# Column sums, head transposes and a part copy put in another order in a hand-scheduled fp32 two-block network

## What is computed

```python
# first block, first mixer
p = (h @ w_in)                    # 256 x 5120, in 10 blocks of 512 columns
f = lb + (1 - lb) * sigmoid(hf)
o_hg = hgrn2_scan(silu(hq), 1 - f, log(f), hi)   # decay exp(bcum_t - bcum_s) for every pair of rows
o_ret = retention_scan(rope(rq), rope(rk) * 128 ** -0.5, rv)
...
# second block
z = h @ w_in                      # 256 x 5120, again 10 blocks of 512 columns
q, k, v, xb, bg, cg, gates = split(z)
q = partial_rope(rms_norm(to_heads(q), g_q), cos, sin)   # 8 heads of 64
k = partial_rope(rms_norm(to_heads(k), g_k), cos, sin)
y_a = moba_attention(q, k, v)
...
x = x + ga2 * hierarchical_moe(h2, ...)   # 32 experts, 6 MB of fp32 weights each
```

## Time and profile before

| | us |
|---|---|
| median of three executions | 1425.47 |
| lowest and highest | 1422.99, 1425.79 |
| the profiled execution, own time | 1423.28 |
| its span, first to last instruction | 1421.5 |
| PE busy (share of the span) | 1229.7 (87%) |
| DVE busy | 651.7 (46%) |
| ACT busy | 245.9 (17%) |
| POOL busy | 59.9 (4%) |
| mean granted clock of TensorE | 0.94 |

### The profile page before, as it was taken

How to read it: one execution, slowest core, us unless ns; L and a number is a source line. 1 busy time by engine, 2 the same in 40 slices (tenths; PEclk the granted TensorE clock), 3 DMA queues, 4 the chain that set the end, 5 groups by cost and what they waited for, 6 DMA issues and landing times.

```text
span 1421.5 us, 15723 instructions
## 1 busy us (share of the span) xinstructions
PE 1229.7 (87%) x6651; PEld 807.0 (57%) x6651; DVE 651.7 (46%) x874; ACT 245.9 (17%) x501; POOL 59.9 (4%) x74
## 2 busy tenths in 40 slices
PE   8999999999999999999999999999674564645647
PEld 5889749994457676997445888655231221312212
DVE  7598326667865754567876764314110100101001
ACT  2331312220012321331002242013000000000000
POOL 1005100000010001000001200000000000000000
PEclk9999999999999999999999999999986887878888
DMA  9533335449953334556993443397999999999997
GB/s 359 179 129 118 119 133 192 158 170 346 350 190 119 118 119 149 178 179 232 348 350 112 167 148 123 130 430 299 424 428 428 428 429 427 428 427 428 428 425 264
DMA packets 94392, 376.98 MB, mean 265 GB/s; under 512 B 7248, under 2 KB 7920, under 8 KB 82416
## 3 DMA queue, kind: packets, MB, share of 16 engines
q1 hardware_dynamic: 93728, 373.84, 67.8%
q0 software_dynamic: 576, 2.10, 0.4%
q10 hardware_dynamic: 16, 0.00, 0.0%
HBM read 374.88 MB, written 1.05 MB: 264 GB/s over the span
## 4 chain that ended last, share of the span: by engine, by line
PE 74%; DMA 21%; DVE 2%; ACT 2%; issue 1%; POOL 0%; DVEq 0%; SPq 0%; ACTq 0%; POOLq 0%
PE PS L740 17%; PE PS L1004 14%; PE PS L957 12%; PE PS L783 9%; DMA weights<-in_w 8%; DMA arena<-in_w 6%; PE PS L1220 6%; DMA proj_rows<-in_w 4%; PE PS L723 4%; PE PS L1258 3%; DMA normalised<-in_w 2%; PE PS L992 2%; PE PS L679 2%; PE PS L865 1%; PE PS L925 1%
## 5 line engine op out<-in xcount | busy, mean ns | idle before, releaser
L740 PE MATMUL PS<-weights,normalised 128*128 128x256 f32 x816 | 182.6, 380 | 2.0 <-DVE weights L1820 1.3
L1220 PE MATMUL PS<-weights,x_rows 128*32 128x512 f32 x368 | 132.4, 726 | 47.1 <-DMA proj_rows<-in_w 25.1
L740 PEld LDWEIGHTS PS<-weights,normalised 128*128 128x128 f32 x816 | 153.8, 190 | 26.3 <-issue 5.1
L1004 PE MATMUL PS<-weights,arena 128*128 128x512 f32 x384 | 167.4, 592 | 0.0
L2420 DVE TENSOR_TENSOR x_rows<-x_rows,PS 128x512 f32<-128x512 f32 x8 | 8.4, 1046 | 289.2 <-PE PS L1220 289.2
L1220 PE MATMUL PS<-arena,x_rows 128*32 128x512 f32 x256 | 95.2, 707 | 39.3 <-DMA weights<-in_w 28.5
L783 PE MATMUL PS<-weights,arena 128*128 128x512 f32 x288 | 125.4, 594 | 2.7 <-ACT arena L1451 1.4
L1004 PEld LDWEIGHTS PS<-weights,arena 128*128 128x128 f32 x384 | 72.9, 190 | 90.8 <-issue 90.8
L1220 PE MATMUL PS<-proj_rows,x_rows 128*32 128x512 f32 x240 | 79.9, 716 | 44.2 <-DMA normalised<-in_w 23.0
L957 PE MATMUL PS<-normalised,weights 128*128 128x128 f32 x896 | 106.9, 275 | 0.0
L957 PEld LDWEIGHTS PS<-normalised,weights 128*128 128x128 f32 x896 | 103.4, 192 | 0.0
(11 more groups left out here) (352 smaller groups left out, 1727.9 us busy)
## 6 DMA issues: line engine op xcount, KB each, us to landing
weights<-in_mlp_w SPq DMA_DIRECT2D x32, 2048.0 KB, 8.5
weights<-in_w SPq DMA_DIRECT2D x32, 2048.0 KB, 34.3
arena<-in_w SPq DMA_DIRECT2D x24, 2048.0 KB, 35.9
proj_rows<-in_w SPq DMA_DIRECT2D x16, 2048.0 KB, 34.2
weights<-in_ev_w_in SPq DMA_DIRECT2D x10, 2048.0 KB, 8.4
weights<-in_w_in SPq DMA_DIRECT2D x10, 2048.0 KB, 7.8
proj_rows<-in_w_ada SPq DMA_DIRECT2D x16, 1024.0 KB, 11.0
early_weights<-in_w SPq DMA_DIRECT2D x8, 2048.0 KB, 37.5
```

The lines of the kernel that those rows point to most:

```text
L740: last = mm(at, lhs[:, k, :], rhs[:, k, :], start=(first and k == 0), stop=(k == 3), skip_group_check=not first)
L1004: last = mm(PS[:, bank, :], lhs[:, k0 + i, rows], rhs[:, i, :], start=(g == 0 and i == 0), stop=(g == NGRP - 1 and i == 1))
L1220: last = mm(PS[CAP * x:CAP * (x + 1), 4 + kind, :], XG[:, k, CAP * x:CAP * (x + 1)], w[:, k, :], start=(k == 0), stop=(k == KT - 1), tile_ ...
```

## The change

Two places are touched.

In the second block PE's wait for `qk_ready` and the 16 transposes go from ahead of block 4 into it, between its sixth and its last product. On DVE `col_sums` of block 4 goes from behind `qk_ready` to behind the first scaling of tile 1, ahead of the rest of its rotation. On ACT `finish` of block 3 and the four parts of block 4 go ahead of the four copies to `T2`.

In the first mixer part 0 of block 4 goes ahead of `level_exp(1)` on ACT.

No instruction is added or left out, and no transfer is changed.

```diff
-            def seven_block(b):
+            def seven_block(b, ahead_of_last=None):
...
                 product(z, HT[:, 4:8, 0:P], b21, True).then_inc(sem("proj_part"), 1)
+                if ahead_of_last:
+                    ahead_of_last()
                 pe.wait_ge(sem("part_read"), 4 * m + 4)
                 pe.wait_ge(sem("col_sums"), 2 * m + 2)
                 product(x, HT[:, 4:8, P:T], t4, False).then_inc(sem("block_used"), 1)
...
-            pe.wait_ge(sem("qk_ready"), 1)
-            for q in range(4):
-                tt, half = q // 2, q % 2
-                quad(4 + q, [PR[:, tt, (4 * half + j) * P:(4 * half + j + 1) * P] for j in range(4)])\
-                    .then_inc(sem("qk_T_raw"), 1)
-            seven_block(B_IN2_AT[4])
+
+            def queries_T():
+
+                pe.wait_ge(sem("qk_ready"), 1)
+                for q in range(4):
+                    tt, half = q // 2, q % 2
+                    quad(4 + q, [PR[:, tt, (4 * half + j) * P:(4 * half + j + 1) * P] for j in range(4)])\
+                        .then_inc(sem("qk_T_raw"), 1)
+
+            seven_block(B_IN2_AT[4], ahead_of_last=queries_T)
...
                 else:
+                    part(at, 0)
                     level_exp(1)
-                    part(at, 0)
                     part(at, 1)
...
             finish(IN[2], 2 * NB)
+            finish(IN[3], 3 * NB)
+            parts(IN[4])
             for q in range(4):
                 tt, half = q // 2, q % 2
                 act.wait_ge(sem("qk_T_raw"), q + 1)
                 a(T2[:, 4 * half:4 * half + 4, tt * P:(tt + 1) * P],
                   PS[:, 4 + q, :].rearrange("p (h t) -> p h t", h=4), ACT.Copy).then_inc(sem("qk_T"), 1)
-            finish(IN[3], 3 * NB)
-            parts(IN[4])
...
                 link(v.tensor_tensor(qk, qk, colb(ST[:, 128 + 16 * tt:144 + 16 * tt], AD), ALU.mult))
+                if tt:
+                    col_sums(IN[4])
                 for i in range(2):
...
             dve.sem_inc(sem("qk_ready"), 1)
             E0 = EV_IN + OD_IN
-            col_sums(IN[4])
             last_sum(IN[4])
             part_sums(IN[3], 3 * NB)
```

## The result

| | before | changed |
|---|---|---|
| median of 13 runs, us | 1425.78 (1420.6 to 1427.94) | 1428.31 (1426.54 to 1430.81) |
| profiled execution, us | 1423.28 | 1430.81 |
| its span, us | 1421.5 | 1429.0 |
| mean granted clock | 0.940 | 0.933 |

The ratio of the changed kernel to the one before is 1.0026, with a 95% interval of 1.0017 to 1.0036. That is 3.7 us more (2.4 to 5.1), and 2.5 us by the medians. The forecast was +0.7 us and "no change". The kernel is slower, by 2.5 to 3.7 us where 0.7 was forecast.

A forecast was written before the change was run, and what follows sets the result against it. PE was taken to bound the kernel before 960 us, expert weight loads from 1000 us. First mixer -0.4 and fifth block +1.15 gave +0.7 us on the 1425.47 us median: 1426.2 us, "no change", range 1423.5 to 1428.5.

The forecast's parts named there:

- Bound of the kernel: Whole kernel: PE limits before 960 us, expert weight loads from 1000 us; edits worth exactly their change in PE's waits.
- First mixer: Block 4, part 0 copied ahead of first exponential: 0.4 us faster, with a new 0.8 us wait in block 5.
- the higher price of a switch: First mixer, ACT: a table switch of about 2.66 us would make the part 0 edit give nothing; not adopted.
- Second block, the order: Fifth block of the projection: PE waits 2.7 us for part 0 and does the transposes afterwards; 1.15 us slower.
- Second block, the pace behind the pause: Fifth block, after PE's wait: five products 8.63 us, restart 0.1, transposes 1.75, with granted clock 1.00.
- my first rival: Fifth block: the pause lets the clock fall, costing some 2.3 us more; sum +3.0, 1428.5 us; chance 6%.
- my own 0.7 for the rest: Both edits together: -0.4 us in the first mixer and +1.15 us in the fifth block, without a clock fall.
- My condition for it: Fifth block: a 2.7 us pause lowers the clock and PE is slow for over about 4.3 us behind it.
- Rival 2: Fifth block: PE does not wait, needing part 0 ahead of finish or part_sums 2.7 us earlier; -1.7 us, chance 8%.

## Why the prediction was wrong

The size was missed by one term, and with it the verdict "no change". Point by point:

- **Bound of the kernel.** Right: what PE lost or gained before 960 us went through to the end, +2.52 us by two stretches and +2.53 by the medians (with a scatter of over 1 us). The traces say it once more: in the thirteen executions the first logits start anywhere from 824.26 to 834.01 us, and from there to the end it is 592.1 to 594.9 us. A late start is nowhere made good. But the edits are not "worth exactly what they take from, or add to, PE's waits": PE's pace is a second quantity, and it moved.
- **First mixer.** Right in size and in kind: 0.41 us in place of 0.4, with the new wait in block 5 where I put it (0.67 us; I wrote about 0.8), and the kernel with part 3 ahead of the second exponential shows that this wait was the cap. The first exponential made nothing late. The table load was again 1.28 us with the exponential right behind it (74.00 and 75.29 in the changed kernel), so the higher price of a switch, 2.66 us, did not show.
- **Second block, the order.** Right: block 4 starts at once, the pause is there (2.51 us of idle time, for which my count gave 2.7), ACT releases it, and transposes done behind it in place of ahead of it cost 1.24 us, against 1.15.
- **Second block, the pace behind the pause.** This is the step that failed: "Then follow five products (8.63), a restart (0.1)". I took the products at the full clock, and wrote "The granted clock is 1.00 there". The four products that come first took 8.70 us and not 7.0, at 1.2 GHz for most of 3.4 us: **+1.69 us that the sum did not have**. With the pause filled the same four take 7.01 us, which shows that the pause is the cause.
- **The rival.** This outcome was my first rival, at 6%. I priced it at 2.3 us from the earlier trace rows, that is from the place where the clock recovers after a wait of over 10 us; it cost 1.7. With my own 0.7 for the rest that makes +2.4, and with the 0.41 and 1.24 that were measured it makes +2.5. My condition for it, PE slow for more than about 4.3 us, was too strict: it was slow for 3.4.
- **Why it got only 6%.** "The clock stays at 1.00" up to 1000 us was a wrong reading of the kernel before. It is at 0.55 from 482.00 to 485.50 and at 0.56 and 0.50 from 755.00 to 762.00, with PE busy throughout. The slices of the page show a 9 there, since a fall of a few microseconds is lost in a slice of 35.5. And rows between 1.3 and 10 us of idle time were there to be read, in the expert stage:

```profile
1014.58 0.85 PE L1220 MATMUL PS<-arena,x_rows 128*32 128x512 f32 x2 [5.13 <-DMA weights<-in_w]
```

```profile
1014.00:1018.00 4.00, 3.42 (x20) 1.27 (x24) 0.00 (x0) 0.00 (x0) 0.00 (x0) 0.61 0.99 426
1018.00:1022.00 4.00, 4.00 (x42) 1.42 (x36) 0.00 (x0) 0.00 (x0) 0.00 (x0) 0.97 1.00 426
```

  Behind 5.13 us the clock lost 0.39 of 4 us and 0.03 of the next 4, which is 1.7 us: the price that the fifth block then paid. Behind 3.21 us (at 1054.55) it fell too, and behind 2.52, 2.30, 2.18 and 1.80 it did not. By these rows a pause of 2.7 us lies between a length without a fall and one with it, so the chance should have been far above 6%, and the price 1.7 us. The Trainium skill ("TensorE: Matmul & The Clock Gate", section "Loop structure matters more than you think") says that long waits between matmuls bring the slow clock back; the trace agrees, with 0.54 behind 2.51 us, and here the rule was worth more than I let it be.
- **Rival 2, no wait in the fifth block**, needed part 0 ahead of `finish`. The experiment that puts it there reached 58.91, so the condition was named rightly.
- **What can be told apart.** I took 0.2% from the scatter of three runs. That was too coarse for thirteen runs a side: the interval was 0.2% wide in all, 0.1% to either side, and a difference of 2.5 us was told from none both times. Two comparisons of the kernel before with itself were off by 0.1%, so about 0.1% is what such a comparison can tell.

## What to carry to other kernels

What a wait on PE costs is more than its own length: in the fifth block waits of 1.3 and 1.66 us left the clock alone, and one of 2.5 us was followed by 3.4 us at about half of it. Look for the granted clock behind every wait and every run of very small matmuls, in windows of a few microseconds; idle time alone doesn't show it, nor do the slices of the page. When work is moved out of a gap in PE's stream, ask what fills the gap afterwards, and put the longest remaining pause at a price of its own. And when a copy that PE waits for stands behind an instruction that waits for a third engine, move the copy out first; reordering the rest around it moves the wait and does not end it.

## What the runs showed of the hardware that I had not expected

- In the fifth block a pause of 1.66 us left the granted clock at 1.00; pauses of 2.51 and 3.04 us were followed by about 3.4 us at or near half, and cost 1.69 and about 1.7 us each time they occurred. In the expert stage 45 waits of 1.71 to 2.75 us cost nothing of the clock. Three needless products in the pause, 2.7 us of additional work on PE, made the kernel faster by 1.69 us in its stretch.
- The clock is a source of scatter between executions by itself. From the end of stretch A to the start of stretch B no edit of this document touches anything, and no wait of PE is longer than 1.3 us. That part took 618.4 us in the two executions with 3.4 us at half clock in it, 620.1 with 6.8 us (one execution), 621.2 to 621.7 with 10.2 us (eight) and 623.4 with 13.7 us (two). So every 3.4 us at half clock cost some 1.7 us, as in the fifth block.
- Another part of the scatter arises at the start. PE's first matmuls of the first projection in the kernel before and in the changed one:

```profile
11.48 1.96 PE L723 MATMUL PS<-weights,normalised 128*128 128x512 f32 x4 [0.35 <-issue]
```

```profile
12.93 3.69 PE L723 MATMUL PS<-weights,normalised 128*128 128x512 f32 x4 [1.80 <-issue]
```

The same four records take 1.96 or 3.69 us, so they run at full or at about half pace. The granted clock reads 1.00 in both, so that the clock is the reason is not shown. In the three profiles of the kernel before they start up to 1.7 us apart (11.48, 13.16 and 12.87), and it begins its cumulative sums at 64.66, 68.02 and 66.05 us. No edit lies ahead of that point. So two spans of one execution each can differ by 3.4 us before anything differs in the code, and the profiled 1429.0 against 1421.5 shows three times the true difference: of the 7.5 us, 3.2 arise ahead of stretch A and 1.9 behind stretch B.
